# A two-layer hybrid attention trunk on one Trainium2 core: the last two output chunks made by positions

## The reference

```python
for l in range(DEPTH):                                   # DEPTH = 2
    h = rms_norm(x, norm_g[l])
    q_a, kv_a, g_a, z_a, q_b, k_b, v_b, f_b, z_b, merge = split(h @ w_in[l])
    y_a = nsa_mixer(q_a, kv_a, g_a, ...) * silu(z_a)     # compressed, selected and window attention
    y_b = fox_mixer(q_b, k_b, v_b, f_b, ...) * silu(z_b) # attention with forget gates
    merged = sigmoid(r_a) * (y_a @ w_nsa[l]) + sigmoid(r_b) * (y_b @ w_fox[l])
    x = x + merged @ w_out[l]
return x * rsqrt(mean(x * x, -1) + 1e-6) * final_g
```

## Time and profile before

| what | before |
|---|---|
| median of 3 runs | 1476.54 us |
| the profiled execution | 1476.18 us |
| its span, first to last instruction | 1474.1 us |
| PE busy | 1464.6 us (99%) |
| DVE / ACT / POOL busy | 1032.0 / 903.9 / 485.1 us |
| PE's granted clock, mean | 0.999 of full speed |

### The profile page before, as it was taken

The page is one execution under the profiler, slowest core; times in us unless marked ns, Lnnn a source line. Parts: engine busy times, 40 slices in busy tenths (PEclk is TensorE's granted clock), DMA queues, the critical chain, the costliest instruction groups (busy, mean ns, idle before and its releaser), DMA issues.

```text
span 1474.1 us, 24870 instructions
## 1 busy us (share of the span) xinstructions
PE 1464.6 (99%) x7654; PEld 1236.5 (84%) x7654; DVE 1032.0 (70%) x2401; ACT 903.9 (61%) x1886; POOL 485.1 (33%) x578
## 2 busy tenths in 40 slices
PE   9999999999999999999999999999999999999998
PEld 7888888888888888888888888888888888888887
DVE  6888878777778874434578877778787787643444
ACT  5776777777777752223466777777777776522233
POOL 1435536445445310000023446445445353000000
PEclk9999999999999999999999999999999999999999
DMA  9222222112222143333463112222212222433332
GB/s 281 68 64 58 58 57 58 52 50 58 57 57 58 44 140 90 98 100 88 111 182 89 53 49 58 57 58 58 58 45 57 56 58 58 143 93 102 90 100 86
DMA packets 213890, 117.85 MB, mean 80 GB/s; under 512 B 9304, under 2 KB 212400, under 8 KB 213296
## 3 DMA queue, kind: packets, MB, share of 16 engines
q1 hardware_dynamic: 211408, 107.49, 26.6%
q0 software_dynamic: 1728, 8.66, 1.6%
q10 hardware_dynamic: 672, 0.70, 0.1%
HBM read 110.41 MB, written 6.42 MB: 79 GB/s over the span
## 4 chain that ended last, share of the span: by engine, by line
PE 95%; ACT 2%; DMA 2%; DVE 1%; issue 0%; POOL 0%; SPq 0%; ACTq 0%; POOLq 0%; DVEq 0%
PE acc L1713 66%; PE o_pair L1793 8%; PE turned L1773 7%; PE scores L1765 4%; PE scores L1764 4%; PE misc L1804 1%; DMA w_raw<-in_w_in_dram 1%; PE acc L2003 1%; DMA w_raw<-in_w_proj_fox_dram 1%; PE misc L1736 1%; PE o_pair L1819 1%; PE turned L1908 0%; PE misc L1812 0%; DMA x_nat<-in_x_dram 0%; ACT w_hi L741 0%; ACT q_swap L772 0%
## 5 line engine op out<-in xcount | busy, mean ns | idle before, releaser
L1713 PE MATMUL acc<-u_hi,w_hi 128*128 128x512 f32 x1096 | 433.1, 395 | 0.1
L1713 PE MATMUL acc<-u_lo,w_hi 128*128 128x512 f32 x1096 | 431.9, 394 | 0.0
L1713 PE MATMUL acc<-u_hi,w_lo 128*128 128x512 f32 x1096 | 429.4, 394 | 0.0
L870 ACT ACTIVATE prob<-prob,row_max 128x128 f32<-128x128 f32 (+3 forms) x384 | 215.2, 560 | 183.2 <-DVE row_max L1311 180.8
L1135 DVE TENSOR_TENSOR w_lo<-w_raw,w_hi 128x1024 fp32r<-128x1024 f32 x188 | 234.8, 1249 | 79.9 <-ACT w_hi L741 78.3
L666 POOL TENSOR_SCALAR prob<-prob,row_inv,gates 128x128 f32<-128x128 f32 (+3 forms) x256 | 171.0, 668 | 327.7 <-DVE row_inv L1318 326.8
L741 ACT ACTIVATE w_hi<-w_raw 128x1024 fp32r<-128x1024 f32 x188 | 197.9, 1053 | 105.0 <-PE acc L1713 91.0
L1713 PEld LDWEIGHTS acc<-u_hi,w_hi 128*128 128x128 f32 x1096 | 205.9, 188 | 39.6 <-DVE w_lo L1135 0.3
L1713 PEld LDWEIGHTS acc<-u_hi,w_lo 128*128 128x128 f32 x1096 | 206.1, 188 | 38.4
L1713 PEld LDWEIGHTS acc<-u_lo,w_hi 128*128 128x128 f32 x1096 | 205.9, 188 | 37.4 <-issue 0.2
L1311 DVE CUSTOM_DVE_ANT_0 prob<-scores,causal 128x128 f32<-128x128 f32 (+3 forms) x384 | 185.0, 482 | 42.7 <-PE scores L1765 32.5
(11 more groups left out here) (244 smaller groups left out, 2283.5 us busy)
## 6 DMA issues: line engine op xcount, KB each, us to landing
w_raw<-in_w_in_dram SPq DMA_DIRECT2D x140, 512.0 KB, 3.7
w_raw<-in_w_proj_nsa_dram SPq DMA_DIRECT2D x16, 512.0 KB, 3.9
w_raw<-in_w_proj_fox_dram SPq DMA_DIRECT2D x16, 512.0 KB, 3.8
w_raw<-in_w_out_dram SPq DMA_DIRECT2D x16, 512.0 KB, 3.9
x_scratch<-xT POOLq DMA_DIRECT2D x2, 2048.0 KB, 11.1
xT<-x_scratch POOLq DMA_DIRECT2D x2, 2048.0 KB, 8.8
x_nat<-in_x_dram SPq DMA_DIRECT2D x4, 512.0 KB, 7.4
c_w<-in_cmp_w_k_dram SPq DMA_DIRECT2D x4, 512.0 KB, 6.5
```

Of the source, the lines that this page charges most:

```text
L870: act.activation(prob[:, ring, 0:width], prob[:, ring, 0:width], ACT.Exp, bias=row_max[:, ring:ring + 1], scale=-1.0, accum_out=row_sum[:, ...
L1713: ins = pe.matmul((bank or acc[par])[0:width, :], w[:, par, k, 0:width], rhs, start=(n == 0), stop=(n == 23))
```

## The change

Chunks 6 and 7 are now made by tiles of 128 positions. `last_piece(qt)` loads 128 positions of `m_hi` or `m_lo` as the stationary operand and streams 256 output features of the weights, so that the result is positions by features at once. For this the split weights of units 6 and 7 must lie side by side: units 4 to 7 are split into `u_hi` and `u_lo` (`late_high`, `late_low`), 128 columns each. The old x of these two chunks is turned early by PE (`turn_x_late`, 8 turns after unit 1) and copied into `o_nat`. The sums of squares of chunks 0 to 5 are taken once for all positions (`early_sums`); those of the last 256 features come from ACT's row sum. The final gain of these features is loaded as rows (`gain_late`) and multiplied in with the scaling. Each tile then goes through residual, square with row sum, root, inverse and scaling by itself; ACT scales columns 0 to 511, DVE 512 to 1023. Tiles 0 to 2 are stored whole, tile 3 in two halves from SP and ACT. The turns and sums at the end, and the loop over `last_piece(h, p)`, are gone.

The diff, cut to what is added; what is removed stands in the functions above. First the transfers and ACT:

```diff
+        gain_late_landed = sem("gain_late_landed")
+        LATE, HALF = P * (KT - 2), D // 2
+        late_banks = [o_pair, acc[0], acc[1], o_pair]
...
+
+        def late_out(u):
+
+            return slice(P * (u - KT // 2), P * (u - KT // 2) + P)
+
+        def x_late(h):
+
+            return o_nat[:, 2 * h:2 * h + 2, LATE:D], scores[h][:, :].rearrange("p (q c) -> p q c", q=2)
...
+            sp.dma_start(gain_late, final_g[LATE:D].unsqueeze(0).broadcast_to([P, 2 * P])
+                         ).then_inc(gain_late_landed, 16)
+            for qt in range(QT - 1):
+                sp.wait_ge(o_scaled[0], 2 * qt + 2)
+                sp.wait_ge(o_scaled[1], qt + 1)
                 sp.dma_start(out[0, qt * P:(qt + 1) * P, :], o_nat[:, qt, :]).then_inc(o_stored, 16)
...
+            sp.wait_ge(o_scaled[0], 2 * QT)
+            sp.dma_start(out[0, T - P:T, HALF:D], o_nat[:, QT - 1, HALF:D]).then_inc(o_stored, 16)
+            sp.wait_ge(o_stored, 16 * (QT + 1))
...
+            def late_high(u):
+                half, par = out0 + u // 2, u % 2
+                act.wait_ge(w_landed[par], 16 * (half + 1 - elsewhere[0]))
+                act.activation(u_hi[:, :, late_out(u)], w_raw[:, par, :, :], ACT.Copy).then_inc(w_hi_done, 1)
+
+            def last_square(qt):
+                act.wait_ge(last_x, qt + 1)
+                act.wait_ge(sq_added, (KT - 1) * (DEPTH - 1) + KT - 3)
+                act.activation(squares[:, qt % 2, 0:2 * P], o_nat[:, qt, LATE:D], ACT.Square,
+                               accum_out=squared[:, qt:qt + 1]).then_inc(last_sq, 1)
+
+            def last_root(qt):
+                act.wait_ge(var_done, DEPTH + 1)
+                act.wait_ge(last_sq, qt + 1)
+                act.activation(rstd_t[:, qt:qt + 1], squared[:, qt:qt + 1], ACT.Sqrt, scale=1.0 / D,
+                               bias=early_mean[:, qt:qt + 1]).then_inc(std_done, 1)
+
+            def last_scale(qt):
+                act.wait_ge(rstd_t_done, DEPTH + qt + 1)
...
-                act.activation(o_nat[:, qt, 0:LATE], o_nat[:, qt, 0:LATE], ACT.Copy, scale=rstd_t[:, qt:qt + 1]
+                act.activation(o_nat[:, qt, 0:HALF], o_nat[:, qt, 0:HALF], ACT.Copy, scale=rstd_t[:, qt:qt + 1]
                                ).then_inc(o_scaled[1], 1)
...
+            split_hi(out0, 1)
+            table_of_sqrt()
+            split_hi(out0 + 1, 0)
+            normed(0)
+            split_hi(out0 + 1, 1)
+            normed(1)
+            act.wait_ge(x_late_turned, 1)
+            act.activation(*x_late(0), ACT.Copy).then_inc(x_late_copied[0], 1)
+            late_high(4)
+            normed(2)
+            landed_out(0)
+            late_high(5)
+            late_high(6)
+            normed(3)
+            late_high(7)
+            normed(4)
+            landed_out(2)
+            normed(5)
+            landed_out(4)
+            for qt in range(QT):
+                last_square(qt)
+                last_root(qt)
+                last_scale(qt)
+            act.wait_ge(o_scaled[1], QT)
+            act.dma_start(out[0, T - P:T, 0:HALF], o_nat[:, QT - 1, 0:HALF]).then_inc(o_stored, 16)
```

DVE:

```diff
+            def late_low(u):
+                half, par = out0 + u // 2, u % 2
+                dve.wait_ge(w_hi_done, 2 * half + par + 1)
+                dve.tensor_tensor(u_lo[:, :, late_out(u)], w_raw[:, par, :, :], u_hi[:, :, late_out(u)],
+                                  ALU.subtract).then_inc(w_lo_done, 1)
+
+            def last_residual(qt):
+                dve.wait_ge(x_late_copied[qt // 2], 1)
+                dve.wait_ge(last_mm, qt + 1)
+                dve.tensor_tensor(o_nat[:, qt, LATE:D], o_nat[:, qt, LATE:D], late_banks[qt][:, 0:2 * P], ALU.add
                                   ).then_inc(last_x, 1)
...
+            def last_inverse(qt):
+                dve.wait_ge(std_done, DEPTH + qt + 1)
+                dve.reciprocal(rstd_t[:, qt:qt + 1], rstd_t[:, qt:qt + 1]).then_inc(rstd_t_done, 1)
+
+            def last_scale(qt):
+                dve.wait_ge(rstd_t_done, DEPTH + qt + 1)
...
-                dve.tensor_scalar(o_nat[:, qt, 0:LATE], o_nat[:, qt, 0:LATE], rstd_t[:, qt:qt + 1], None, ALU.mult
+                dve.tensor_scalar(o_nat[:, qt, HALF:LATE], o_nat[:, qt, HALF:LATE], rstd_t[:, qt:qt + 1], None, ALU.mult
                                   ).then_inc(o_scaled[0], 1)
...
+                dve.wait_ge(gain_late_landed, 16)
+                dve.scalar_tensor_tensor(o_nat[:, qt, LATE:D], o_nat[:, qt, LATE:D], rstd_t[:, qt:qt + 1], gain_late,
+                                         ALU.mult, ALU.mult).then_inc(o_scaled[0], 1)
+
+            split_lo(out0, 1)
+            residual(0)
+            split_lo(out0 + 1, 0)
+            normed(0)
+            residual(1)
+            split_lo(out0 + 1, 1)
+            normed(1)
+            dve.wait_ge(x_late_turned, 1)
+            dve.tensor_copy(*x_late(1)).then_inc(x_late_copied[1], 1)
+            residual(2)
+            late_low(4)
+            normed(2)
+            late_low(5)
+            residual(3)
+            late_low(6)
+            normed(3)
+            landed_out(1)
+            late_low(7)
+            residual(4)
+            normed(4)
+            residual(5)
+            landed_out(3)
+            normed(5)
+            last_residual(0)
+            landed_out(5)
+            dve.wait_ge(last_summed, 1)
+            dve.tensor_scalar(early_mean[:, :], misc[:, 0:QT], 1.0 / D, EPS, ALU.mult, ALU.add).then_inc(var_done, 1)
             last_inverse(0)
             last_scale(0)
...
+            for qt in range(1, QT):
+                last_residual(qt)
+                last_inverse(qt)
+                last_scale(qt)
```

PE:

```diff
-                    ins = pe.matmul((bank or acc[par])[0:width, :], w[:, par, k, 0:width], rhs,
+                    own_w = w[:, par, k, 0:width] if place is None else (u_lo if which == 2 else u_hi)[:, k, place]
+                    ins = pe.matmul((bank or acc[par])[0:width, :], own_w, rhs,
...
+                def turn_x_late():
+
+                    pe.wait_ge(x_back, 16 * DEPTH)
+                    for qt in range(QT):
+                        for p in range(2):
+                            first = 2 * P * (qt % 2) + P * p
+                            ins = pe.transpose(scores[qt // 2][:, first:first + P],
+                                               xT[:, KT - 2 + p, P * qt:P * qt + P], ident[:, :])
+                    ins.then_inc(x_late_turned, 1)
...
+                               free=(m_part, 2 * KT * (l + 1) + 1 + k) if k < 2 else (x_done, X_DVE + KT * l + k - 1),
+                               place=late_out(k) if l + 1 == DEPTH and k >= KT // 2 else None)
+                    if l + 1 == DEPTH and k == 1:
+                        turn_x_late()
                     if l + 1 == DEPTH and k > 1:
                         turn_out(k - 2)
...
+            def last_piece(qt, first=0, last=24):
+                cols = slice(P * qt, P * qt + P)
                 for n in range(first, last):
                     k, which = divmod(n, 3)
...
+                    if n == 0 and qt == 0:
+                        pe.wait_ge(w_lo_done, 2 * (half0 + U_OUT // 2) + KT + 2)
+                    if n == 0 and qt in (1, 2):
+                        pe.wait_ge(x_done, X_DVE + KT * (DEPTH - 1) + KT - 4 + qt)
+                    if n == 0 and qt == 3:
+                        pe.wait_ge(last_x, 1)
+                    ins = pe.matmul(late_banks[qt][:, 0:2 * P], (m_lo if which == 1 else m_hi)[:, k, cols],
+                                    (u_lo if which == 2 else u_hi)[:, k, 2 * P:4 * P], start=(n == 0), stop=(n == 23))
                     if n == 23:
                         ins.then_inc(last_mm, 1)
...
+            def early_sums():
+                pe.wait_ge(sq_added, (KT - 1) * (DEPTH - 1) + KT - 3)
+                for qt in range(QT):
+                    ins = pe.matmul(misc[:, qt:qt + 1], sq_sum[:, P * qt:P * qt + P], ones[:, 0:1],
+                                    start=(qt == 0), stop=(qt == QT - 1), skip_group_check=True)
                 ins.then_inc(last_summed, 1)
...
-            last_piece(0, 0)
+            last_piece(0)
             turn_out(KT - 4)
-            last_piece(0, 1)
+            last_piece(1, 0, 12)
             turn_out(KT - 3)
-            last_piece(1, 0, 0, 14)
-            last_sums(0)
-            last_piece(1, 0, 14)
-            last_turns(0)
-            last_piece(1, 1)
-            last_sums(1)
-            last_turns(1)
+            early_sums()
+            last_piece(1, 12)
+            last_piece(2)
+            last_piece(3)
 # ---- launch: one core; inputs and outputs as the reference has them ----
```

More of the change, by code:

```diff
@@ L1078, in landed_out @@
                                    ACT.Copy).then_inc(o_copied[k % 2], 1)
-                for k in range(KT if l + 1 < DEPTH else KT - 2):
-                    split_hi(out0 + (k + 1) // 2, (k + 1) % 2)
-                    if k:
-                        normed(k - 1)
```

(77 more changed lines are left out.)

78 lines of the change are left out of this document (5 added, 73 removed).

## The result

| what | before | changed |
|---|---|---|
| median of 8 runs each, same chip | 1476.51 us | 1481.50 us |
| lowest to highest | 1475.89 to 1476.83 | 1480.74 to 1482.31 |
| span of the profiled execution | 1474.1 us | 1479.3 us |

The ratio is 1.0035, with a 95% interval of 1.0026 to 1.0045: 5.0 us slower, where 1.7 us faster was forecast. 1481.5 is also the number of rival 3. But the signs named for it are absent, as the rows show.

A forecast was written before the change was run, and what follows sets the result against it. TensorE, 95% of the chain, was taken as the bound. Last matmul 1467.1 + tail 2.24 + store 3.06 = span end 1472.4 against 1474.1, -1.7 us: median forecast 1474.8 us, range for 8 in 10 1473.8 to 1475.9.

The forecast's parts named there:

- rival 3: Late matmuls: TensorE's weight loads are not hidden under 256-column matmuls, 6.7 us, giving 1481.5 us; chance 0.05.
- the signs named for it: Signs of being wrong on late matmuls: pitch over 120 ns; weight loads not hidden, 188 ns against a 118 ns pitch.
- TensorE's queue: Matmuls, turns and sums up to the last matmul: 1.23 us removed, 1.56 added, net +0.3, between +0.2 and +0.6.
- the early sums: Four single-column fp32 matmuls added on TensorE, each going as two: 0.68 us, or 0.9 by another row.
- The supply of weights: Loads and splits for units 4 to 7 cost nothing; least slack 4.5 us, units 6 and 7 together 7.2 us.
- The tail: From last matmul to the last store's issue: 2.24 us where 3.73 stood, bounds 1.9 and 2.5.
- The scaling: Last step of a tile's chain: ScalarE's 512 columns 0.71 us, VectorE's two parts 0.26 + 0.43 = 0.69, at most 0.91.
- The store: From the last store's issue to the span's end: 3.06 us where 3.60 stood, with only tile 3's 512 KB left.
- Rival 1: Last store gets no shorter, 3.60 us, because latency and not bytes sets it: 1475.3 us; chance 0.10.
- rival 2: Last tile's two store queues run side by side, 0.66 us less: 1474.1 us; chance 0.04.
- Rival 4: Tile 2's chain is late and its store stands before tile 3's: up to 1.3 us, 1476.1 us; chance 0.03.
- for what I have not seen: Chance of 0.01 for unseen causes, within the 0.06 given to being slower by over 2.95 us.

The follow-up runs named there:

- the changed kernel in the old places: Changed kernel with `early_mean` sharing the 32 bytes of `squared`, so all other tiles lie where they lay before the change: 1474.68 us, ratio 0.9988.
- the run with one store: Changed kernel with aligned tiles, its last tile stored in one 512 KB transfer from SP instead of two of 256 KB: 1469.87 us against 1469.27.
- the last scan: Kernel without the computation, units of 24 matmuls of 512 columns with operand places varied, also between neighbours: plain 64 bytes 229.0 ns, 96 bytes 233.5 ns.

## Why the prediction was wrong

It failed in its first paragraph, at the sentence "The change leaves everything up to the second layer's output projection alone". True of the instructions, it is false of their addresses. Every step that builds on the trace of before inherits it: the last matmul ended at 1473.71 and not at 1467.1, of which the place accounts for all but some tenths: 5.9 us stood before the first changed instruction of TensorE, and from there to the last matmul it took 38.20 us where the changed kernel in the old places takes 37.65. The step that failed is thus a term put at nothing: what the new tile's place does to matmuls that the diff doesn't touch. The runs show 6.8 us in its place: the changed kernel has 1481.50 us with its own places and 1474.68 with the old ones (two sets of runs, in which the kernel before had 1476.51 and 1476.31). That the number met rival 3 is chance: it priced the loads of the late matmuls, and these hold 119 ns.

The other steps can be read in the changed kernel with old places. From the 768th matmul of the long stretch to the end of the span it has 1473.4 - (1254.68 + 175.55) = 43.2 us; before it was 1474.1 - (1254.07 + 768 x 0.2286) = 44.5. The forecast's -1.7 is -1.3 there and -1.6 in the medians; its 1474.8 was 1474.68. The terms below miss by 0.4 us together, so that the median comes within 0.1 is partly luck.

- **TensorE's queue**, +0.33 forecast: from the 768th matmul to the end of the last, 37.65 us against 37.15, +0.5. Eight turns took 0.88, as said; the early sums 0.79, not 0.68. They stand as x8, so that an fp32 matmul that is no turn goes as two is right.
- **The supply of weights**: right, in the changed kernel itself. ScalarE waited 2.76 us for the load of unit 6 (below), and unit 7's low part was done at 1453.50, 7.0 us before the first late group; 7.2 was forecast.

```profile
1448.19 1.06 ACT L1102 ACTIVATE u_hi<-w_raw 128x1024 fp32r<-128x1024 f32 x1 [2.76 <-DMA w_raw<-in_w_out_dram]
...
1452.27 1.23 DVE L1650 TENSOR_TENSOR u_lo<-w_raw,u_hi 128x1024 fp32r<-128x1024 f32 x1 [0.56 <-ACT u_hi L1102]
```

- **The tail**, 2.24 forecast: 2.43 us from the last matmul to the issue. Square with sum 0.52 and inverse 0.17 as said, root 0.30 for 0.28. The scaling is 0.75 for 0.71: ScalarE's branch takes 0.72 and VectorE's is a little longer, with 354 ns for 256 columns in SBUF, where I took 260, and 479 with the gain, for 430, of which some 80 overlap (below, changed kernel). The other 0.1 is hand-offs.

```profile
L1667 DVE TENSOR_SCALAR o_nat<-o_nat,rstd_t x4: 354/354/355, 1467.2 to 1475.4; 128x256 f32<-128x256 f32 x4
L1670 DVE SCALAR_TENSOR_TENSOR o_nat<-o_nat,rstd_t,x_nat x4: 478/479/480, 1467.5 to 1475.7; 128x256 f32<-128x256 f32 x4
```

- **The store**, 3.06 forecast: 3.1 us from issue to end, and in the changed kernel the stretches above carry 4 + 471 + 49 KB in 1.4 us, where 1.3 to 1.6 was given. Rival 1 (3.60) falls, and rival 2 by the run with one store. Rival 4 too: tile 2's store was issued 2.8 us ahead of tile 3's, 1467.53 against 1470.31.

The chance of 0.01 "for what I have not seen" was too small. It was read off the columns of the instructions; no row of the profile shows where a tile lies.

## What to carry to other kernels

A new tile, however small, moves every tile declared behind it; before calling a difference the work of the change, run the kernel before with the same shift. On a kernel that TensorE bounds with fp32 matmuls of 512 columns, let moving and loaded tiles all start at the same byte modulo 256: here that was worth 5.1 us of 1476, three times the change itself. Small tiles put into one place give the room for such a shift.

## What the runs showed that I had not expected

- A matmul of 128 x 512 in fp32r takes 226.7 ns from start to start where all moving and loaded operands start at one place modulo 256 bytes, and 228 to 238 elsewhere. At 384 columns (173 to 177 ns) and 256 (117 to 120) 0 has no such gain.
- The loss is not spread evenly. The three matmuls of one chunk of the contraction took 226, 229 and 232 ns at 64 bytes and 232, 237 and 231 at 96, in the last scan as in the kernel. Such a repeating pattern, with nothing waited for, is how it looks in a trace.
